# Chunks of x turned between the products of the first two weight blocks, low halves on POOL, y in four buffers

## What is computed

```python
def rmsnorm(x, g):
    r = lax.rsqrt(jnp.mean(x32 * x32, axis=-1, keepdims=True) + EPS)
    return (x32 * r * g)
xn = rmsnorm(x, g_attn_norm)              # (288, 2048)
z = jnp.einsum('bsd,de->bse', xn, w_in)   # blocks 0 to 3 of 128 columns: query latent, 4 to 7: kv latent, ...
```

## Time and profile before

| | |
|---|---|
| three runs | 2946.59, 2946.97, 2951.3 us, median 2946.97 |
| profiled execution, device time | 2953.18 us |
| its span | 2951.4 us (1.8 us lie around it) |
| PE busy | 2896.2 us, 98% of the span |
| DVE, ACT, POOL busy | 48%, 39%, 4% |
| PE turns the chunks 3 to 15 | 16.15 to 28.93 us |
| high halves of blocks 0 and 1 | 28.93 to 39.36 us |
| low halves of blocks 0 and 1 | from 39.36 us, 4.40 us |

### The profile page before, as it was taken

How to read it: one execution, slowest core, us unless ns; L and a number is a source line. 1 busy time by engine, 2 the same in 40 slices (tenths; PEclk the granted TensorE clock), 3 DMA queues, 4 the chain that set the end, 5 groups by cost and what they waited for, 6 DMA issues and landing times. The chain is left out here.

```text
span 2951.4 us, 49867 instructions
## 1 busy us (share of the span) xinstructions
PE 2896.2 (98%) x19398; PEld 2699.2 (91%) x19398; DVE 1429.4 (48%) x2174; ACT 1138.8 (39%) x1875; POOL 104.9 (4%) x346
## 2 busy tenths in 40 slices
PE   8998999999999998999999999999999999999999
PEld 7865898888898896899999999999999999999999
DVE  4465433333333332355555434445667654667644
ACT  5535332332332231344444333334444433444433
POOL 0100000000000000000000000002100000000100
PEclk9998999999999998999999999999999999999999
DMA  6522301001001102756565655556555556555464
GB/s 204 208 80 88 106 1 33 17 17 33 29 5 33 33 1 93 208 157 197 171 186 173 189 171 160 167 151 199 165 163 164 162 148 175 172 170 161 145 180 129
DMA packets 620546, 372.13 MB, mean 126 GB/s; under 512 B 23928, under 2 KB 602050, under 8 KB 619336
## 3 DMA queue, kind: packets, MB, share of 16 engines
q1 hardware_dynamic: 608200, 357.63, 40.6%
q10 hardware_dynamic: 11824, 11.50, 1.1%
q0 software_dynamic: 368, 0.81, 0.1%
HBM read 347.16 MB, written 22.75 MB: 125 GB/s over the span
## 5 line engine op out<-in xcount | busy, mean ns | idle before, releaser
L287 DVE TENSOR_TENSOR w_lo_b<-stage,w_hi_b 128x2048 fp32r<-128x2048 f32 (+1 forms) x289 | 619.2, 2143 | 425.0 <-ACT w_hi_b L280 424.9
L299 PE MATMUL bank<-xnH,w_hi_b 128*128 128x288 f32 x2784 | 756.2, 299 | 6.3 <-PEq L191 6.3
L300 PE MATMUL bank<-xnL,w_hi_b 128*128 128x288 f32 x2784 | 750.9, 296 | 0.0
L280 ACT ACTIVATE w_hi_b<-stage 128x2048 fp32r<-128x2048 f32 (+1 forms) x289 | 517.9, 1792 | 572.4 <-PE bank L304 536.8
L299 PEld LDWEIGHTS bank<-xnH,w_hi_b 128*128 128x128 f32 x2784 | 524.5, 188 | 15.9 <-issue 15.3
L300 PEld LDWEIGHTS bank<-xnL,w_hi_b 128*128 128x128 f32 x2784 | 524.2, 188 | 0.3
L1524 PE MATMUL bank<-ukH,latH 128*128 128x384 f32 (+2 forms) x1280 | 458.0, 358 | 0.0
L1526 PE MATMUL bank<-ukH,latL 128*128 128x384 f32 (+2 forms) x1280 | 452.4, 353 | 0.0
L1525 PE MATMUL bank<-ukL,latH 128*128 128x384 f32 (+2 forms) x1280 | 452.0, 353 | 0.0
L1755 DVE TENSOR_REDUCE rk<-sq_n 128x3 f32<-128x384 f32 (+1 forms) x320 | 184.9, 580 | 508.3 <-ACT sq_n L1679 508.3
L304 PE MATMUL bank<-xnH,w_lo_b 128*128 128x288 f32 x2784 | 396.6, 295 | 0.0
(11 more groups left out here) (471 smaller groups left out, 2786.1 us busy)
## 6 DMA issues: line engine op xcount, KB each, us to landing
stage<-in_w_in_dram SPq DMA_DIRECT2D x88, 1024.0 KB, 5.0
stage<-in_w_up_dram SPq DMA_DIRECT2D x88, 1024.0 KB, 5.3
stage<-in_w_down_dram SPq DMA_DIRECT2D x64, 704.0 KB, 4.5
latf<-in_cache_kv_latent_dram SPq DMA_DIRECT2D x64, 256.0 KB, 2.5
stage<-in_w_branch_a_dram SPq DMA_DIRECT2D x16, 1024.0 KB, 5.6
stage<-in_w_branch_b_dram SPq DMA_DIRECT2D x16, 1024.0 KB, 5.4
stage<-in_w_out_dram SPq DMA_DIRECT2D x16, 1024.0 KB, 5.6
stage<-in_w_uk_dram SPq DMA_DIRECT2D x8, 1024.0 KB, 5.0
```

The costliest lines, as they stand in the source:

```text
L280: act.activation(h, a, ACT.Copy).then_inc(w_hi, 1)
L287: dve.tensor_tensor(lo, a, h.bitcast(F32), ALU.subtract).then_inc(w_lo, 1)
L299: pe.matmul(out, hi, xH(k), start=first and k == 0, stop=False)
L300: pe.matmul(out, hi, xL(k), start=False, stop=False)
```

## The change

Four things are changed, all in this first stage.

1. PE turns chunks 3 to 6 before the products and the others in between: after the products of chunks k and k+1 (k even) it turns chunks k+7 and k+8, as far as there are any.
2. Four banks (4, 5, 6 and 2) take the chunks in turn instead of three; `turn_x(c)` waits for the copy and also for y of chunk c-4.
3. y goes into four buffers, `yx`, which lie in `c_tok` (free at that time) instead of two in `y_x`, and DVE makes y from the bank instead of from `xT`. It still waits for the copy.
4. POOL makes the low halves. DVE makes y only, and both `split_lo` come after y of chunk 15.

```diff
+            yx = c_tok[:].rearrange("p t c -> p (t c)")[:, 0:4 * T].rearrange("p (k t) -> p k t", k=4)
...
                     def turn_x(c):
-                        need(pe, x_cp, c - 2)
+                        need(pe, x_cp, c - 3)
+                        need(pe, x_y, c - 3)
                         for t, (t0, n) in enumerate(TILES):
-                            tr = pe.transpose(bank[4 + c % 3][:, t0:t0 + n], x_tok[0:n, t, c * P:(c + 1) * P], ident[0:n, 0:n])
+                            tr = pe.transpose(bank[(4, 5, 6, 2)[c % 4]][:, t0:t0 + n], x_tok[0:n, t, c * P:(c + 1) * P], ident[0:n, 0:n])
...
-                    for c in range(3, KC):
-                        turn_x(c)
...
-                    for k in range(KC):
-                        pe.wait_ge(x_L, k + 1)
-                        for n in range(2):
-                            if k == 0:
-                                pe.wait_ge(w_hi, n + 1)
-                            half(n, k)
+                    for c in range(3, 7):
+                        turn_x(c)
+                    for k in range(0, KC, 2):
+                        for c in range(k, k + 2):
+                            pe.wait_ge(x_L, c + 1)
+                            for n in range(2):
+                                if c == 0:
+                                    pe.wait_ge(w_hi, n + 1)
+                                half(n, c)
+                        for c in range(k + 7, min(k + 9, KC)):
+                            turn_x(c)
...
-                        act.activation(xT[:, c, :], bank[4 + c % 3][:, 0:T], ACT.Copy).then_inc(x_cp, 1)
+                        act.activation(xT[:, c, :], bank[(4, 5, 6, 2)[c % 4]][:, 0:T], ACT.Copy).then_inc(x_cp, 1)
...
-                        act.activation(xnH[:, c, :], y[:, c % 2, :], ACT.Copy).then_inc(x_H, 1)
+                        act.activation(xnH[:, c, :], yx[:, c % 4, :], ACT.Copy).then_inc(x_H, 1)
...
                 def _(pool):
+                    for c in range(KC):
+                        pool.wait_ge(x_H, c + 1)
+                        pool.tensor_tensor(xnL[:, c, :], yx[:, c % 4, :], xnH[:, c, :].bitcast(F32), ALU.subtract).then_inc(x_L, 1)
...
-                    def low(c):
-                        dve.wait_ge(x_H, c + 1)
-                        dve.tensor_tensor(xnL[:, c, :], y[:, c % 2, :], xnH[:, c, :].bitcast(F32), ALU.subtract).then_inc(x_L, 1)
                     for c in range(KC):
                         dve.wait_ge(x_cp, c + 1)
-                        need(dve, x_L, c - 1)
-                        dve.scalar_tensor_tensor(y[:, c % 2, :], xT[:, c, :], vec[:, G_ATTN + c:G_ATTN + c + 1], rb[:], ALU.mult, ALU.mult).then_inc(x_y, 1)
-                        if c >= 1:
-                            low(c - 1)
-                        if c == 12:
-                            split_lo(dve, At(0))
-                    low(KC - 1)
+                        need(dve, x_L, c - 3)
+                        dve.scalar_tensor_tensor(yx[:, c % 4, :], bank[(4, 5, 6, 2)[c % 4]][:, 0:T], vec[:, G_ATTN + c:G_ATTN + c + 1], rb[:], ALU.mult, ALU.mult).then_inc(x_y, 1)
+                    split_lo(dve, At(0))
                     split_lo(dve, At(1))
```

## The result

Fifteen runs of each kernel on one chip: the changed kernel takes 2956.79 us (median), the one before 2947.63. The ratio is 1.0026, 95% interval 1.0019 to 1.0034, so the change costs 5.6 to 10 us. I had forecast +4.3, with 2954.5 as the upper end.

What follows compares the result with a forecast made beforehand. PE, busy for 98% of the span, was taken as the bound; first-stage high halves ending at 43.4 to 43.9 instead of 39.36 us gave +4.3, so 2946.97 + 4.3 = 2951.3 us, range 2945.5 to 2954.5.

Steps and rivals of the forecast that it cites:

- The first product: First stage on PE: the first high product can start at 19.9 us, after chunks 3 to 6 are turned.
- the hole to 21.3 before block 1's weights: First stage on PE: PE stands from about 20.4 to 21.6 us, as block 1's `w_hi` is ready only at 21.53.
- chunk 15 turned at 38.7: Alternation on PE at the low clock: the turn of chunk 15 ends at 38.4 us, leaving 24 unbroken products.
- no slow first use of POOL: POOL's first subtraction: a first use beyond 1.6 us would add one for one, up to +8.7 us; argued against.
- the mechanism that would hold POOL: End of first stage: DVE's first `split_lo`, two inputs in SBUF, starts at 39.3 and holds POOL until 41.6 us.
- the alternation by itself loses time by the low clock: First stage on PE: 38 products and 9 turns at the low clock cost +4.0 to +4.6 us, taken as +4.3.
- the end of the stage: POOL's last low half comes at 42.3 us, PE asks for it at 43.2: hidden, with 0.9 us to spare.
- A third: PE's clock rises 4.0 to 5.2 us after the unbroken products begin, at 42.4 to 43.6 us.
- the mixture kept the level that it met: Two attention stretches mixing transposes and products kept their clock, full or 0.50; so the alternation stays at the low clock.
- D: Rival, chance 0.1: POOL is slow; with every low half at 2.15 us the high halves end +14.7 us.
- B: Rival, chance 0.15: the clock rises late in the alternation, at 36.5 to 40 us, giving +2.7 to +3.4 us.
- C: Rival, chance 0.2: the mixture brings up the clock between 26.5 and 33 us, giving -1.8 to +1.1 us.

Runs made afterwards that it cites:

- a2: The changed kernel with the low halves back on DVE and the first weight subtraction after chunk 12; ratio to the kernel before 1.0014.
- c3: The changed kernel with only ACT's order changed: from chunk 7 on, the high half of chunk c-1 right behind the copy of c; ratio to the kernel before 1.0003.
- a4: The changed kernel with DVE's two weight subtractions moved early, after y of chunks 8 and 10; ratio to the kernel before 1.0010.
- a3: The changed kernel with ACT making the high half of chunk c before the copy of chunk c+3; ratio to the kernel before 1.0029.
- c2: The changed kernel with c3's order on ACT and both weight subtractions early as in a4; ratio to the kernel before 0.9994.
- b4: a4 with 16 added unused matmuls of constants on PE before x arrives; ratio to the kernel before 1.0011.
- b5: b4 with 6 more added matmuls before the rms and 6 more before the first product; ratio to the kernel before 1.0005.
- c1: c2 with 9, 5, 1 and 1 added unused matmuls before x, the rms, the first product and block 1's first product; ratio to the kernel before 0.9996.

## Why the prediction was wrong

**Right.** The first product, the hole to 21.3 before block 1's weights, the rhythm of 0.24 and 1.73 us for two chunks, chunk 15 turned at 38.7 (38.4 forecast), POOL's subtraction (0.77 a piece, 0.81 forecast), no slow first use of POOL (its first two subtractions took 1.55 us together), the mechanism that would hold POOL (DVE's weight subtractions), and that the alternation by itself loses time by the low clock. Its size was less than I said: in a2, with no late low half at all, it is 3.3 us, where I had 4.0 to 4.6. The other 6.5 us of the changed kernel's 9.8 are its two waits (3.6), what the lost clock took (an estimate: 12 high products and some 9 low ones at 0.24 instead of 0.133 us, 2.2) and some 0.7 that stays unassigned.

**The step that failed** is the one on the end of the stage: "the last low half comes at 41.6 + 0.7 = 42.3", and "hidden, with 0.9 us to spare". It counted chunk 15 alone as late. I had said that PE turns at least five chunks ahead of its products and concluded that no other engine sets the pace. But ACT's queue makes the high half of chunk c only after the copy of chunk c+3. Before the change that copy was long done or soon to come; in the alternation it waits for PE's turn of chunk c+3, which PE does late. So the high halves of chunks 12 to 15 all came behind the turn of chunk 15 (39.09 to 40.5), four low halves met both weight subtractions, and the last ended at 46.8 instead of 42.3. The diff doesn't touch ACT's order; what changed is the meaning of its waits. I had read the order of PE, DVE and POOL after the change, but not the order of ACT again. Shown by: c3 (ACT's order alone, waits 3.6 to 1.66), a4 (port free, 7.16 to 3.09 us) and a2.

**A second term** was missing behind it: the clock was lost again. In the changed kernel it fell at 43.45, right after the wait of 2.00 us that ended at 43.27, and in a3 at 42.59, after the wait of 2.01 us that ended at 42.11; in a4, c2 and c3, with no wait over 1.66 us there, it stayed up. That the wait brought it down is argued from these cases; no run varies the wait alone. It made 3.6 us of waiting into about 5.8.

**A third** was mis-sized and erred the other way, so that it hid part of the miss: "In two starts of unbroken products it rose 4.0 us ... and ... 5.2 us ... after the first. I take the same here". It rose 1.4 us after the first unbroken product in the changed kernel and 1.3 in a2, and before the first in a3, a4, c2 and c3. So the alternation was not without effect on when the clock rises, as I had taken it to be. My reading of the earlier trace rows, "the mixture kept the level that it met", was too short already: the first stretch was read up to 275.00, and the clock fell at 275.41, after a wait of PE of 1.89 us in that same mixture.

**The rivals.** Of D (POOL slow) only the smaller form came true: POOL's operation is fast and was held at the end. B and C held that the clock rises before my 42.4. With PE's order unchanged it rose at 27.67 (c3, C's case), 35.77 to 36.03 (a3, a4, c2, between C's 33 and B's 36.5) and 40.03 to 40.04 (a2 and the changed kernel, B's upper end), never where I had it. The 3.3 us of a2 are B's number (+2.7 to +3.4). So B was right about the clock in the changed kernel, and 0.35 for B and C together was, if anything, too little. What decides when it rises in one execution stays open; the six kernels have the same order on PE up to there, and from 16 us on its waits are alike to 0.11 us.

## What to carry to other kernels

When work is moved within one engine's queue, walk every other queue again in its own order: an unchanged "copy of c+3, then high half of c" became a wait for the last turn. Look at what is behind it at the end of the loop, where a lag of three chunks comes out all at once. Two-input operations in SBUF should not be put on DVE and POOL for the same stretch where one of them is waited for, and a hole of 2 us on PE can cost more than itself: here the clock was lost after it, in two kernels of two.

## What the runs showed of the hardware

- POOL's two-input subtractions of 128x288 come 0.77 us apart alone, and one that meets a DVE subtraction of 128x2048 takes 2.84 us (four in 7.16 us beside two of those, in 3.09 us without). DVE is held as well: the two subtractions took 2.90 and 2.87 us in the changed kernel, where one alone takes 2.29. From the bank, DVE's y takes 0.52 us beside POOL's subtraction; with both inputs in SBUF 1.05.
- With the same work on PE the granted clock rose anywhere between 27.67 and 40.04 us in six kernels whose alternation began at about 21.3. After chunk 15, a wait of 2.0 us was followed by its fall in two of two kernels, one of 1.66 in none of one. Around the turning of chunks 3 to 6 it fell after much less: in b4, b5 and c1 no wait of PE near it was longer than 0.60 us.
- The record of the granted clock shows a full clock for the first 33 us of the kernel before, where the starts of the products from 29.33 on, 0.24 us apart, say 1.2 GHz: the starts are the better witness there.
